# The last stage of a float32 decoder trunk: where h is turned token-major

## The chip, the cores and the metric

The kernel runs on one core of a Trainium2 chip. The metric is the device time of one execution in microseconds (us). Three runs of the kernel before took 1103.12 to 1103.98, median 1103.35.

## The reference, cut to what matters

Two layers over 512 tokens of 1024 features, in float32: differential attention or multi-scale pooling, a gated MLP with a short convolution, and a gated per-layer embedding. The change is in the last of these, together with the final norm:

```
for i in range(DEPTH):
    ...
    h = h + conv_glu_ffn(rmsnorm(h, ffn_norm_g[i]), w_up[i], conv_w[i], conv_b[i], w_down[i])
    gate = jax.nn.sigmoid(rmsnorm(h, ple_norm_g[i]) @ w_ple_gate[i])
    h = h + gate * (p[i] @ w_ple_proj[i])
return rmsnorm(h, final_norm_g)
```

## The kernel before, in words

The order of each engine's instructions is written by hand; semaphores join the engines. Through most of the kernel h is feature-major: `h[:, k, :]` holds 128 features (partitions) of tile k for all 512 tokens. Every product is made of three TensorE instructions (lines 1257 to 1259): the high parts, and each low part with the other's high part. Weights come in units of 128x1024 float32 into four slots (`w_raw`, loaded from SyncE, line 340); ScalarE makes the high part (`split_hi`, line 392), VectorE the low part (`split_lo`, line 821).

The last down phase of the MLP (`residual_phase("down12", ...)`) adds eight tiles to h. For each tile VectorE makes the low part of a coming weight unit (line 821), adds the result to h (line 1038), makes the low part of the normed input of the tile before (`x_low`, line 829) and adds its squares up (`sum_squares`, line 856). ScalarE makes the input's high part and the squares between them.

The last stage is different: its output is token-major. The gate product has 128 tokens as rows and 512 of the 1024 output features as columns, and it runs in two halves of the features. In the first half k, the tile of input features, is the outer loop, and the four token tiles t share the banks 0 to 3: 8 steps of 4 x 3 = 12 matmuls. After k = 1 stand the token sums of the norm (`norm_sums`, line 1277). In the second half t is the outer loop; the last t is cut into two pieces of 256 columns. The stage's weights are 8 units, TAIL to TAIL+7. To add h, it must be token-major as well: `h_tok`, eight pieces of 128 tokens by 512 features. `token_transposes` (line 1628) makes each with four TensorE transposes of 128x128 into a bank, ScalarE copies it to SBUF (line 683).

Behind the products ScalarE makes the sigmoid (`gate`, line 704), VectorE multiplies it with the embedding (`gated`, line 1207) and adds `h_tok` (line 1209), ScalarE sums the squares (lines 711, 718), GpSimd makes the inverse root (lines 806 to 810), and VectorE scales and multiplies with the gain (`final`, line 1220), from where SyncE stores. For the last token tile the gain is multiplied in early (line 1230), and ScalarE scales (line 752). GpSimd has done nothing else since the pooling masks at 244 us. It has issued transfers only in the attention (lines 779 and 783).

`h_tok` lies over the buffers `g_hi` and `g_lo`, which the down phase reads.

Of the kernel before, what the change touches and what calls it, by code (L numbers as in the profile page):

```python
# [8 lines left out]
F32 = mybir.dt.float32  # L9
# [24 lines left out]
PLE_KT = PLE_DIM // P  # L34
POOL_KT = D_MODEL // len(POOL_WINDOWS) // P
GROUP = SEQ // P
N_GROUPS = N_HEADS // GROUP
ROW_HEADS = N_HEADS - 2
FFN_PARTS = (8, 8, 6)
# [57 lines left out]
def hybrid_trunk(nc, gain_and_x0, xT, pT, weights, final_gain, columns, out, o_rows):  # L97
    with ExitStack() as ctx:
        def sem(name):
            return ctx.enter_context(nc.semaphore(name))  # L100

        def sb(name, shape, dt, scope=ctx):
            return scope.enter_context(nc.sbuf_tensor(name, shape, dt))
# [19 lines left out]
        p_raw = sb("p_raw", [P, DEPTH * PLE_KT, SEQ], F32, product)  # L123
        product.close()
        product = ExitStack()
        h_tok = sb("h_tok", [P, 2 * TT, SEQ], F32, product)
        product.close()
        g_hi = sb("g_hi", [P, KT, SEQ], F32R)
        g_lo = sb("g_lo", [P, KT, SEQ], F32R)
# [44 lines left out]

        gain_b = sb("gain_b", [P, D_MODEL], F32, ffn)
        G = len(POOL_WINDOWS)
        band32 = sb("band32", [P, G, BAND], F32, ffn)
        edge32 = sb("edge32", [P, G, EDGE], F32, ffn)
        band = sb("band", [P, G, BAND], F32R, ffn)
        first_band = sb("first_band", [P, G, BAND], F32R, ffn)  # L180
        edge_lo = sb("edge_lo", [P, G, EDGE], F32R, ffn)
        mlp = ExitStack()
        u32 = sb("u32", [P, 2, PAD + SEQ], F32, mlp)
        c32 = sb("c32", [P, 2, SEQ], F32, mlp)
# [48 lines left out]
            sem("band_one"), sem("band_below"), sem("band_set"), sem("band_diff"), sem("band_done"), sem("edge_done"))  # L233
        z_mm, zhi_done, zlo_done, pool_mm = sem("z_mm"), sem("zhi_done"), sem("zlo_done"), sem("pool_mm")

        h_T, h_copied, gate_mm, gate_done, gated_done, h_added = (
            sem("h_T"), sem("h_copied"), sem("gate_mm"), sem("gate_done"), sem("gated_done"), sem("h_added"))
        first_sq, second_sq, last_sq, token_total, token_var, frms_done, finv_done, gain_in, gained_done = (
            sem("first_sq"), sem("second_sq"), sem("last_sq"), sem("token_total"), sem("token_var"), sem("frms_done"),
            sem("finv_done"), sem("gain_in"), sem("gained_done"))  # L240
# [83 lines left out]
        def z_bank(i):  # L324

            return bank[4 + (i + 1) % 3]

        WO_BANKS = (1, 0, 7, 3)
        WT_BANKS = [(0, 512), (512, 384), (896, 384)]
# [53 lines left out]
        def _(act):  # L383
# [294 lines left out]
                add_pool_bias(KT - 1)  # L678


            def tokens_copy(m):
                act.wait_ge(h_T, m + 1)
                act.activation(h_tok[:, m, :], bank[4 + m % 3][:, :], ACT.Copy).then_inc(h_copied, 1)

            gates = [g32, s32]

            tables = iter(range(104, 116))
# [18 lines left out]
            def first_square(t):  # L706

                act.wait_ge(h_added, t + 1)
                if t:
                    act.wait_ge(first_sq, t)  # L710
                act.activation(u32[:, 0, 0:SEQ], h_tok[:, t, :], ACT.Square, accum_out=first_sum[:, t:t + 1]).then_inc(first_sq, 1)

            def second_square(t):

                act.wait_ge(h_added, TT + t + 1)
                if t:
                    act.wait_ge(second_sq, t)
                act.activation(u32[:, 1, 0:SEQ], h_tok[:, TT + t, :], ACT.Square,
                               accum_out=second_sum[:, t:t + 1]).then_inc(second_sq, 1)

            split_hi(TAIL + 2)
            split_hi(TAIL + 3)
            rms_of(NORM_PLE1)
            split_hi(TAIL + 4)
            for m in range(4):
                tokens_copy(m)
            split_hi(TAIL + 5)
            for m in range(4, 8):
                tokens_copy(m)
            split_hi(TAIL + 6)  # L730
            table(ACT.Sigmoid)
            act.wait_ge(icol_done, NORM_PLE1 + 1)
# [25 lines left out]
        def _(pool):  # L758
# [38 lines left out]
            for mat, width in ((band32, BAND), (edge32, EDGE)):  # L797

                for g, win in enumerate(POOL_WINDOWS):
                    pool.affine_select(out=mat[:, g, :], in_=mat[:, g, :], compare_op=ALU.is_ge, fill=0.0, base=win - 1,  # L800
                                       pattern=[[-1, width]], channel_multiplier=1).then_inc(band_set, 1)

            for t in range(TT - 1):
                pool.wait_ge(first_sq, t + 1)
# [9 lines left out]
        def _(dve):  # L814
            def split_lo(n, a=0):

                if n >= N_UNITS:
                    return
                s, w = slot_of(n), blocks_of(n) * P
                dve.wait_ge(hi_done, SLOTS * a + n + 1)  # L820
                dve.tensor_tensor(w_lo[s][:, 0:w], w_raw[s][:, 0:w], w_hi[s][:, 0:w].bitcast(F32),  # L821
                                  ALU.subtract).then_inc(lo_done, 1)
# [28 lines left out]
            def sum_squares(norm, m):  # L851
                n_sq = KT * norm + m
                dve.wait_ge(sq_done, n_sq + 1)
                if m:
                    dve.wait_ge(acc_done, n_sq)
                    dve.tensor_tensor(acc[:, :], acc[:, :], sq[:, n_sq % 2, :], ALU.add).then_inc(acc_done, 1)
                else:
                    dve.tensor_copy(acc[:, :], sq[:, n_sq % 2, :]).then_inc(acc_done, 1)
# [178 lines left out]
            def residual_add(m, src):  # L1037
                dve.tensor_tensor(h[:, m, :], src, h[:, m, :], ALU.add).then_inc(evac_done, 1)  # L1038

            def residual_phase(name, norm, layer, which, look=LOOK):  # L1040
                for m in range(KT):
                    n = PHASES[name][0] + m
                    if m + look < KT + LOOK:
                        split_lo(n + look)
                    dve.wait_ge(unit_done, n + 1)
                    residual_add(m, bank[WO_BANKS[m % SLOTS] if name == "wo" else m % SLOTS][:, :])
                    if norm is not None and m > 0:
                        x_low(norm, m - 1, gain(layer, which, m - 1))
                        sum_squares(norm, m - 1)
                if norm is not None:  # L1050
                    x_low(norm, KT - 1, gain(layer, which, KT - 1))
                    sum_squares(norm, KT - 1)
# [142 lines left out]

            split_lo(TAIL + 2)
            split_lo(TAIL + 3)
            inverse(NORM_PLE1)
            for n in range(4, 8):
                split_lo(TAIL + n)  # L1200
# [2 lines left out]
            def gated(i):  # L1203

                m, cols = PIECES[i]
                dve.wait_ge(gate_done, i + 1)
                dve.tensor_tensor(c32[:, i % 2, cols], emb[:, m, cols], gates[i % 2][:, cols], ALU.mult).then_inc(gated_done, 1)  # L1207
                dve.wait_ge(gated_done, i + 1)
                dve.tensor_tensor(h_tok[:, m, cols], c32[:, i % 2, cols], h_tok[:, m, cols], ALU.add).then_inc(h_added, 1)  # L1209

            def last_square(i, before, into):

                m, cols = PIECES[i]
                dve.wait_ge(h_added, i + 1)
                dve.tensor_tensor_reduce(c32[:, i % 2, cols], h_tok[:, m, cols], h_tok[:, m, cols], 1.0, before,
                                         ALU.mult, ALU.add, into).then_inc(last_sq, 1)

            def final(m, cols=slice(0, SEQ)):
                half, t = divmod(m, TT)
                dve.scalar_tensor_tensor(out=emb[:, m, cols], in0=h_tok[:, m, cols], scalar=final_inv[:, t:t + 1],  # L1220
                                         in1=gain_b[:, half * SEQ + cols.start:half * SEQ + cols.stop],
                                         op0=ALU.mult, op1=ALU.mult).then_inc(y_dve, 1)

            dve.wait_ge(h_copied, 2 * TT)
            dve.wait_ge(emb_done, DEPTH * KT)
            for t in range(TT):
                gated(t)
            dve.wait_ge(gain_in, 16)
            dve.wait_ge(h_added, TT)
            dve.tensor_tensor(emb[:, TT - 1, :], h_tok[:, TT - 1, :], gain_b[:, 0:SEQ], ALU.mult).then_inc(gained_done, 1)  # L1230
            for t in range(TT - 1):
                gated(TT + t)
                if t == TT - 2:
# [17 lines left out]
        def _(pe):  # L1251
# [365 lines left out]
                return exact(dst, [((x_hi[:, k, TOK[t]], x_lo[:, k, TOK[t]]), (w_hi[s][:, w], w_lo[s][:, w]), no_wait)],  # L1617
                             start=k == 0, stop=k == KT - 1)

            def token_transposes(m):  # L1620

                half, t = divmod(m, TT)
                if m >= 3:
                    pe.wait_ge(h_copied, m - 2)
                else:
                    pe.wait_ge(emb_done, DEPTH * KT)
                for j in range(TT):
                    last = pe.transpose(bank[4 + m % 3][:, j * P:(j + 1) * P], h[:, half * TT + j, TOK[t]], ident[:, :])
                last.then_inc(h_T, 1)

            for k in range(KT):
                pe.wait_ge(lo_done, TAIL + k // 2 + 1)
                pe.wait_ge(x_ready, KT * NORM_PLE1 + k + 1)
                for t in range(TT):
                    if k == 0:
                        pe.wait_ge(evac_done, result_of("down12", TT + t))
                    done = gate_product(bank[t][:, :], 0, k, t)
                    if k % 2 and t == TT - 1:
                        done.then_inc(unit_done, 1)
                    elif k == KT - 1:  # L1640
                        done.then_inc(gate_mm, 1)
                if k == 1:
                    norm_sums(NORM_PLE1)
                if 2 <= k < 6:
                    token_transposes(2 * k - 4)
                    token_transposes(2 * k - 3)

            pe.wait_ge(h_copied, 2 * TT)
            pe.wait_ge(rms_done, NORM_PLE1 + 1)
            for t in range(TT - 1):  # L1650
                for k in range(KT):
# [93 lines left out]
```

## Time and profile before

| | us |
|---|---|
| median of three runs | 1103.35 |
| profiled execution | 1103.46 |
| its span, first to last instruction | 1101.7 |
| TensorE busy in the span | 1089.8 (99%) |
| VectorE busy | 719.2 (65%) |
| ScalarE busy | 515.0 (47%) |
| GpSimd busy | 25.2 (2%) |

Busy time is no time on the path. What sets the end is read from the chain that ended last, and what an engine waits for from the idle time ahead of an instruction. Matmuls overlap in the pipeline, so their durations add up to more than the time between their starts. The granted clock of TensorE was 0.998 of full speed.

### The profile page before, as it was taken

The page shows a single profiled execution, that of the slowest core. Times are in us where ns is not written, and L with a number is a line of the kernel's source. Part 1 is how long each engine was busy: PE and PEld are TensorE (multiplying, and loading weights), DVE is VectorE, ACT ScalarE, POOL GpSimd, SP SyncE. Part 2 cuts the span into 40 slices and gives each one's busy share as a digit, 9 for nine tenths or more (in the row PEclk, how much of TensorE's full clock was granted, in tenths as well). Part 3 has the DMA queues.
Part 4 walks back from the last instruction along what each step waited for, and adds up shares of the span by engine and source line. Part 5 has one row for each costly group of instructions (what it writes and reads, how often), then busy time and mean ns, then how long its engine had stood idle before and what let it go on. Part 6 is the DMA issues. An engine that isn't in the chain of part 4 may idle for free.

```text
span 1101.7 us, 14447 instructions
## 1 busy us (share of the span) xinstructions
PE 1089.8 (99%) x5152; PEld 908.5 (82%) x5152; DVE 719.2 (65%) x1107; ACT 515.0 (47%) x775; POOL 25.2 (2%) x82
## 2 busy tenths in 40 slices
PE   9999999999999999999999999999999999999997
PEld 8878888888888888888888888888888888888886
DVE  7567878575775377743776778777437773477636
ACT  6456667364643144421445677444314442244554
POOL 0001110020000000000000000000000000000001
PEclk9999999999999999999999999999999999999999
DMA  8213243233233233232233222233322233233411
GB/s 330 62 58 83 62 96 79 65 109 103 92 99 115 77 95 95 96 115 79 95 103 127 95 94 77 77 95 99 114 78 101 95 106 115 77 95 95 134 58 76
DMA packets 31295, 107.88 MB, mean 98 GB/s; under 512 B 3600, under 2 KB 3600, under 8 KB 31248
## 3 DMA queue, kind: packets, MB, share of 16 engines
q1 hardware_dynamic: 30288, 105.13, 30.8%
q0 software_dynamic: 672, 1.59, 0.6%
q8 instruction: 30, 0.49, 0.2%
q10 hardware_dynamic: 288, 0.53, 0.2%
q14 instruction: 17, 0.14, 0.0%
HBM read 105.12 MB, written 2.11 MB: 97 GB/s over the span
## 4 chain that ended last, share of the span: by engine, by line
PE 93%; DVE 4%; ACT 2%; issue 1%; POOL 0%; DVEq 0%; ACTq 0%; POOLq 0%
PE bank L1257 29%; PE bank L1259 29%; PE bank L1258 29%; PE bank L1351 1%; PE bank L1277 1%; DVE w_lo L821 1%; PE bank L1364 1%; DVE probs L943 1%; DVE h_tok L1209 1%; DVE c L1207 0%; ACT probs L494 0%; DVE emb L1220 0%; PE bank L1318 0%; ACT w_hi L392 0%; PE bank L1544 0%
## 5 line engine op out<-in xcount | busy, mean ns | idle before, releaser
L1257 PE MATMUL bank<-x_hi,w_hi 128*128 128x512 f32 x896 | 350.2, 391 | 0.0
L1259 PE MATMUL bank<-x_hi,w_lo 128*128 128x512 f32 x896 | 348.8, 389 | 0.0
L1258 PE MATMUL bank<-x_lo,w_hi 128*128 128x512 f32 x896 | 348.7, 389 | 0.0
L821 DVE TENSOR_TENSOR w_lo<-w_raw,w_hi 128x1024 fp32r<-128x1024 f32 (+1 forms) x189 | 226.0, 1197 | 52.6 <-ACT w_hi L392 52.5
L392 ACT ACTIVATE w_hi<-w_raw 128x1024 fp32r<-128x1024 f32 (+1 forms) x189 | 193.8, 1031 | 109.4 <-PE bank L1259 109.4
L1259 PEld LDWEIGHTS bank<-x_hi,w_lo 128*128 128x128 f32 x896 | 168.2, 188 | 35.0
L1257 PEld LDWEIGHTS bank<-x_hi,w_hi 128*128 128x128 f32 x896 | 168.2, 188 | 34.8 <-issue 0.4
L1258 PEld LDWEIGHTS bank<-x_lo,w_hi 128*128 128x128 f32 x896 | 168.3, 188 | 34.5
L1257 PE MATMUL bank<-g_hi,w_hi 128*128 128x512 f32 x352 | 136.9, 389 | 0.0
L1258 PE MATMUL bank<-g_lo,w_hi 128*128 128x512 f32 x352 | 136.9, 389 | 0.0
L1259 PE MATMUL bank<-g_hi,w_lo 128*128 128x512 f32 x352 | 136.9, 389 | 0.0
L637 ACT ACTIVATE c<-u,params 128x512 f32<-128x512 f32 x88 | 71.8, 816 | 106.7 <-DVE u L1132 106.7
L1132 DVE TENSOR_TENSOR u<-bank,inv 128x512 f32<-128x512 f32 x88 | 60.7, 689 | 92.2 <-PE bank L1259 92.1
L1038 DVE TENSOR_TENSOR gain_and_h<-bank,gain_and_h 128x512 f32<-128x512 f32 x56 | 38.5, 688 | 97.9 <-PE bank L1259 97.9
L644 ACT ACTIVATE g_hi<-g 128x512 f32 (+1 forms) x44 | 27.8, 632 | 118.8 <-DVE g L1148 118.8
L1257 PEld LDWEIGHTS bank<-g_hi,w_hi 128*128 128x128 f32 x352 | 66.1, 188 | 13.8
L1258 PEld LDWEIGHTS bank<-g_lo,w_hi 128*128 128x128 f32 x352 | 66.1, 188 | 13.7
L1259 PEld LDWEIGHTS bank<-g_hi,w_lo 128*128 128x128 f32 x352 | 66.1, 188 | 13.6
L1142 DVE SCALAR_TENSOR_TENSOR c<-u,params,c 128x512 f32<-128x512 f32 x88 | 66.2, 752 | 10.3 <-DVE c L1137 2.1
L1137 DVE SCALAR_TENSOR_TENSOR c<-u,params,c 128x512 f32<-128x512 f32 x88 | 66.0, 750 | 2.3 <-ACT c L637 0.9
L642 ACT ACTIVATE s<-c 128x512 f32<-128x512 f32 x44 | 27.8, 632 | 75.2 <-DVE c L1142 75.2
L1150 DVE TENSOR_TENSOR g_lo<-g,g_hi 128x512 f32 (+1 forms) x44 | 30.5, 693 | 38.1 <-ACT g_hi L644 38.1
(218 smaller groups left out, 1172.7 us busy)
## 6 DMA issues: line engine op xcount, KB each, us to landing
w_raw<-in_weights SPq DMA_DIRECT2D x189, 512.0 KB, 3.5
gain_and_h<-in_xT SPq DMA_DIRECT2D x7, 256.0 KB, 5.6
o_inv<-o_rows POOLq DMA_DIRECT2D x6, 256.0 KB, 4.8
out<-emb SPq DMA_DIRECT2D x3, 512.0 KB, 3.0
p_raw<-in_pT SPq DMA_DIRECT2D x1, 1024.0 KB, 10.0
w_raw<-in_weights SPq DMA_DIRECT2D x2, 256.0 KB, 3.7
gain_b<-in_final_gain SPq DMA_DIRECT2D x1, 512.0 KB, 4.0
gain_and_h<-in_gain_and_x ACTq DMA_DIRECT2D x1, 260.0 KB, 3.6
```

The costliest lines, as they stand in the source:

```text
L392: act.activation(w_hi[s][:, 0:w], w_raw[s][:, 0:w], ACT.Copy).then_inc(hi_done, 1)
L637: act.activation(c32[:, c, :], u32[:, c, PAD:PAD + SEQ], ACT.Identity, scale=tap(layer, 2, j + c * FT), bias=conv_bias(layer, j + c * FT)) ...
L642: act.activation(s32[:, :], c32[:, 0, :], ACT.Silu).then_inc(silu_done, 1)
L821: dve.tensor_tensor(w_lo[s][:, 0:w], w_raw[s][:, 0:w], w_hi[s][:, 0:w].bitcast(F32), ALU.subtract).then_inc(lo_done, 1)
L1038: dve.tensor_tensor(h[:, m, :], src, h[:, m, :], ALU.add).then_inc(evac_done, 1)
L1132: dve.tensor_tensor(u32[:, c, PAD:], bank[2 * v + c][:, :], inv[:, :], ALU.mult).then_inc(evac_done, 1)
L1137: dve.scalar_tensor_tensor(out=c32[:, c, :], in0=u32[:, c, PAD - 1:PAD - 1 + SEQ], scalar=tap(layer, 1, j + c * FT), in1=c32[:, c, :], op0 ...
L1142: dve.scalar_tensor_tensor(out=c32[:, c, :], in0=u32[:, c, PAD - 2:PAD - 2 + SEQ], scalar=tap(layer, 0, j + c * FT), in1=c32[:, c, :], op0 ...
L1150: dve.tensor_tensor(g_lo[:, 2 * a + v, :], g32[:, :], g_hi[:, 2 * a + v, :].bitcast(F32), ALU.subtract).then_inc(glo_done, 1)
L1257: pe.matmul(dst, w1, m1, start=start and i == 0, stop=False)
L1258: pe.matmul(dst, w1, m0, start=False, stop=False)
L1259: last = pe.matmul(dst, w0, m1, start=False, stop=stop and i == len(parts) - 1)
```

## The change

The TensorE transposes and ScalarE's copies are taken out. VectorE transposes each tile of h in 32x32 blocks into a new buffer, `turned`, once it is done; a block lands on the 32 partitions from which it came. GpSimd then issues 16 transfers within SBUF, each of which carries the blocks of one quarter of the partitions (a) that belong to one quarter of the tokens (c) to their partitions. A run is 4 x 32 elements (512 bytes) on the reading side; a transfer has 32 partitions of 8 runs. `h_tok` has another order within a partition, so the sum reads it in runs of 32 elements; it is written to `emb`, which all that follows reads. `turned` takes the place of the pooling masks.

```
+        turned = sb("turned", [P, KT, P // SQUARE, TT, SQUARE], F32, ffn)
...
+        def h_token_major(m, cols):
+            half, t = divmod(m, TT)
+            tiles = slice(half * TT + cols.start // P, half * TT + cols.stop // P)
+            return h_tok[:, :, tiles, t, :].rearrange("p a j x -> p j a x")
...
-            for m in range(4):
-                tokens_copy(m)
             split_hi(TAIL + 5)
-            for m in range(4, 8):
-                tokens_copy(m)
...
+            pool.wait_ge(unit_done, TAIL)
+            pool.wait_ge(h_turned, KT)
+            for c in range(P // SQUARE):
+                for a in range(P // SQUARE):
+                    pool.dma_start(h_tok[c * SQUARE:(c + 1) * SQUARE, a, :, :, :],
+                                   turned[a * SQUARE:(a + 1) * SQUARE, :, c, :, :]).then_inc(h_moved, 16)
...
+            def turn(m):
+                dve.wait_ge(evac_done, result_of("down12", m))
+                dve.transpose(turned[:, m, :, :, :].rearrange("p c t x -> p t c x"), h[:, m, :].rearrange("p (t c x) -> p t c x", t=TT, x=SQUARE)).then_inc(h_turned, 1)
...
                         sum_squares(norm, m - 1)
+                        if norm == NORM_PLE1:
+                            turn(m - 1)
...
             split_lo(TAIL + 3)
+            turn(KT - 1)
             inverse(NORM_PLE1)
...
-                dve.tensor_tensor(h_tok[:, m, cols], c32[:, i % 2, cols], h_tok[:, m, cols], ALU.add).then_inc(h_added, 1)
+                by_tile = "p (j a x) -> p j a x"
+                dve.tensor_tensor(emb[:, m, cols].rearrange(by_tile, a=P // SQUARE, x=SQUARE),
+                                  c32[:, i % 2, cols].rearrange(by_tile, a=P // SQUARE, x=SQUARE),
+                                  h_token_major(m, cols), ALU.add).then_inc(h_added, 1)
...
-            dve.wait_ge(h_copied, 2 * TT)
+            dve.wait_ge(h_moved, 16 * (P // SQUARE) ** 2)
...
-            dve.wait_ge(h_added, TT)
-            dve.tensor_tensor(emb[:, TT - 1, :], h_tok[:, TT - 1, :], gain_b[:, 0:SEQ], ALU.mult).then_inc(gained_done, 1)
+            dve.wait_ge(first_sq, TT)
+            dve.tensor_tensor(emb[:, TT - 1, :], emb[:, TT - 1, :], gain_b[:, 0:SEQ], ALU.mult).then_inc(gained_done, 1)
...
-                if 2 <= k < 6:
-                    token_transposes(2 * k - 4)
-                    token_transposes(2 * k - 3)
-
-            pe.wait_ge(h_copied, 2 * TT)
+            pe.wait_ge(emb_done, DEPTH * KT)
```

VectorE before, from the low part and the residual sum of the last tile to the low parts of the gate's units:

```order
L821 TENSOR_TENSOR w_lo<-w_raw,w_hi 128x1024 [waits hi_done]
L1038 TENSOR_TENSOR gain_and_h<-bank,gain_and_h 128x512 [waits unit_done]
L829 SCALAR_TENSOR_TENSOR x_lo<-gain_and_h,params,x_hi 128x512 [waits xhi_done]
L856 TENSOR_TENSOR acc<-acc,sq 128x512 [waits acc_done,sq_done]
L829 SCALAR_TENSOR_TENSOR x_lo<-gain_and_h,params,x_hi 128x512 [waits xhi_done]
L856 TENSOR_TENSOR acc<-acc,sq 128x512 [waits acc_done,sq_done]
L821 TENSOR_TENSOR w_lo<-w_raw,w_hi 128x1024 [waits hi_done] x2
L846 RECIPROCAL small<-small 128x4 [waits rms_done]
```

And the same place now (lines are some ten further down):

```order
L830 TENSOR_TENSOR w_lo<-w_raw,w_hi 128x1024 [waits hi_done]
L1047 TENSOR_TENSOR gain_and_h<-bank,gain_and_h 128x512 [waits unit_done]
L838 SCALAR_TENSOR_TENSOR x_lo<-gain_and_h,params,x_hi 128x512 [waits xhi_done]
L865 TENSOR_TENSOR acc<-acc,sq 128x512 [waits acc_done,sq_done]
L1052 STREAM_TRANSPOSE turned<-gain_and_h 128x4x4x32 [waits evac_done]
L838 SCALAR_TENSOR_TENSOR x_lo<-gain_and_h,params,x_hi 128x512 [waits xhi_done]
L865 TENSOR_TENSOR acc<-acc,sq 128x512 [waits acc_done,sq_done]
L830 TENSOR_TENSOR w_lo<-w_raw,w_hi 128x1024 [waits hi_done] x2
L1052 STREAM_TRANSPOSE turned<-gain_and_h 128x4x4x32 [waits evac_done]
L855 RECIPROCAL small<-small 128x4 [waits rms_done]
```

Turn 6 stands ahead of the last tile's low part and sum of squares, turn 7 behind the low parts of two weight units; turns 0 to 5 stand one in each tile before.

ScalarE before, from the high part of unit TAIL+4 to the first two sigmoids:

```order
L392 ACTIVATE w_hi<-w_raw 128x1024 [waits unit_done,raw_in2]
L683 ACTIVATE h_tok<-bank 128x512 [waits h_T] x4
L392 ACTIVATE w_hi<-w_raw 128x1024 [waits unit_done,raw_in3]
L683 ACTIVATE h_tok<-bank 128x512 [waits h_T] x4
L392 ACTIVATE w_hi<-w_raw 128x1024 [waits unit_done,raw_in0]
L691 ACT_TABLE_LOAD
L691 ACTIVATE small<-eps 128x1
L392 ACTIVATE w_hi<-w_raw 128x1024 [waits unit_done,raw_in1,icol_done]
L704 ACTIVATE g<-bank,small 128x512 [waits gate_mm]
L704 ACTIVATE s<-bank,small 128x512 [waits gate_mm]
```

Now the eight copies are gone; the order of the rest is kept. On GpSimd the transfers stand behind the masks and ahead of the inverse roots:

```order
L802 AFFINE_SELECT band<-band 128x144 x3
L802 AFFINE_SELECT edge<-edge 128x16 x4
L809 DMA h_tok<-turned 32x8x128 [waits h_turned,unit_done]
L809 DMA h_tok<-turned 32x8x128 x15
L815 TENSOR_TENSOR small<-small 128x1 [waits second_sq,first_sq]
L817 TENSOR_SCALAR small<-small 128x1 [waits token_total]
L819 TENSOR_TENSOR small<-small 128x1 [waits token_var]
```

Nothing of the kernel's own is queued behind them on GpSimd until the first inverse root.

## Rows read from the trace of the kernel before

**Rows 1.** The page's chain that ended last, by engine:

```profile
PE 93%; DVE 4%; ACT 2%; issue 1%; POOL 0%; DVEq 0%; ACTq 0%; POOLq 0%
```

**Rows 2.** The chain in order of time, last stage: start, us, what:

```profile
1054.52 0.87 PE bank L1628 x8
...
1071.86 1.06 ACT w_hi L392
...
1074.09 0.70 DVE c L1207
...
1083.74 0.58 POOL small L810
...
1084.35 1.42 DVE emb L1220 x2
```

**Rows 3.** The line of the transposes: duration ns min/median/max, starts:

```profile
L1628 PE MATMUL bank<-ident,gain_and_h x32: 270/272/273, 1054.4 to 1066.0; 128*128 128x128 f32 x32
```

**Rows 4.** Timeline of TensorE: start, us, engine line op, count, idle before:

```profile
1050.73 0.95 PE L1277 MATMUL bank<-ones,acc 128*128 128x1 f32 x8
...
1051.54 0.48 PE L1257 MATMUL bank<-w_hi,x_hi 128*128 128x512 f32 x1
...
1054.36 1.03 PE L1628 MATMUL bank<-ident,gain_and_h 128*128 128x128 f32 x8
...
1071.58 0.39 PE L1257 MATMUL bank<-w_hi,x_hi 128*128 128x512 f32 x1
...
1074.30 0.39 PE L1257 MATMUL bank<-w_hi,x_hi 128*128 128x512 f32 x1
```

**Rows 5.** VectorE's groups by shape: busy us, mean ns, idle before:

```profile
L821 DVE TENSOR_TENSOR w_lo<-w_raw,w_hi 128x1024 fp32r<-128x1024 f32 x173 | 210.7, 1219 | 41.6 <-ACT w_hi L392 41.6
...
L858 DVE COPY acc<-sq 128x512 f32<-128x512 f32 x6 | 2.5, 420 | 0.0
```

**Rows 6.** Timeline of VectorE, end of the down phase:

```profile
1037.40 0.96 DVE L821 TENSOR_TENSOR w_lo<-w_raw,w_hi 128x768 fp32r<-128x768 f32 x1 [0.79 <-ACT w_hi L392]
...
1046.46 0.68 DVE L1038 TENSOR_TENSOR gain_and_h<-bank,gain_and_h 128x512 f32<-128x512 f32 x1
...
1048.32 0.74 DVE L829 SCALAR_TENSOR_TENSOR x_lo<-gain_and_h,params,x_hi 128x512 fp32r<-128x512 f32 x1
1048.98 0.68 DVE L856 TENSOR_TENSOR acc<-acc,sq 128x512 f32<-128x512 f32 x1
1049.59 2.35 DVE L821 TENSOR_TENSOR w_lo<-w_raw,w_hi 128x1024 fp32r<-128x1024 f32 x2
```

**Rows 7.** Waits of TensorE's loads, 1045 to 1095 us: total, times, longest:

```profile
PEld bank L1257 <- DVE gain_and_h L1038: 0.2, 1, 0.2
```

**Rows 8.** GpSimd's transfers in the attention, by line: issue in ns, landing in us:

```profile
L779 POOL DMA_DIRECT2D o_rows<-small x6: 595/600/752, 85.3 to 171.5; - x6
...
DMA to landing us min/median/max: 1.7/1.7/1.9
...
L783 POOL DMA_DIRECT2D o_inv<-o_rows x6: 536/542/557, 87.5 to 173.5; - x6
...
DMA to landing us min/median/max: 4.4/4.8/5.4
```

**Rows 9.** Busy time by stretch, last three: granted clock, DMA share, GB/s:

```profile
1054.00:1058.00 4.00, 4.00 (x24) 3.33 (x23) 0.26 (x1) 1.09 (x2) 0.00 (x0) 1.00 0.31 119
1058.00:1071.50 13.50, 13.50 (x73) 11.49 (x72) 2.45 (x2) 6.64 (x10) 0.00 (x0) 1.00 0.00 1
```

**Rows 10.** Timelines of VectorE and ScalarE around the early gain:

```profile
1079.60 0.69 DVE L1230 TENSOR_TENSOR emb<-h_tok,gain_b 128x512 f32<-128x512 f32 x1
1080.06 0.19 ACT L711 ACTIVATION_READ_ACCUMULATOR u<-h_tok 128x1 f32 x1
1080.86 0.69 DVE L1207 TENSOR_TENSOR c<-emb,g 128x512 f32<-128x512 f32 x1 [0.57 <-ACT g L704]
```

**Rows 11.** The page's DMA issues: KB each, us to landing:

```profile
w_raw<-in_weights SPq DMA_DIRECT2D x189, 512.0 KB, 3.5
```

More of the change, by code:

```diff
@@ L36 @@
 GROUP = SEQ // P
+SQUARE = 32
 N_GROUPS = N_HEADS // GROUP
@@ L125, in hybrid_trunk @@
         product = ExitStack()
-        h_tok = sb("h_tok", [P, 2 * TT, SEQ], F32, product)
+        h_tok = sb("h_tok", [P, P // SQUARE, KT, TT, SQUARE], F32, product)
         product.close()
@@ L176, in hybrid_trunk @@
         G = len(POOL_WINDOWS)
[L177 to L181, printed above, removed]
+        pooling = ExitStack()
+        band32 = sb("band32", [P, G, BAND], F32, pooling)
+        edge32 = sb("edge32", [P, G, EDGE], F32, pooling)
+        band = sb("band", [P, G, BAND], F32R, pooling)
+        first_band = sb("first_band", [P, G, BAND], F32R, pooling)
+        edge_lo = sb("edge_lo", [P, G, EDGE], F32R, pooling)
+        pooling.close()
+        turned = sb("turned", [P, KT, P // SQUARE, TT, SQUARE], F32, ffn)
         mlp = ExitStack()
@@ L234, in hybrid_trunk @@
         z_mm, zhi_done, zlo_done, pool_mm = sem("z_mm"), sem("zhi_done"), sem("zlo_done"), sem("pool_mm")
-        h_T, h_copied, gate_mm, gate_done, gated_done, h_added = (
-            sem("h_T"), sem("h_copied"), sem("gate_mm"), sem("gate_done"), sem("gated_done"), sem("h_added"))
+        h_turned, h_moved, gate_mm, gate_done, gated_done, h_added = (
+            sem("h_turned"), sem("h_moved"), sem("gate_mm"), sem("gate_done"), sem("gated_done"), sem("h_added"))
         first_sq, second_sq, last_sq, token_total, token_var, frms_done, finv_done, gain_in, gained_done = (
@@ L678, in _ @@
                 add_pool_bias(KT - 1)
-            def tokens_copy(m):
-                act.wait_ge(h_T, m + 1)
-                act.activation(h_tok[:, m, :], bank[4 + m % 3][:, :], ACT.Copy).then_inc(h_copied, 1)
             gates = [g32, s32]
@@ L710, in first_square @@
                     act.wait_ge(first_sq, t)
-                act.activation(u32[:, 0, 0:SEQ], h_tok[:, t, :], ACT.Square, accum_out=first_sum[:, t:t + 1]).then_inc(first_sq, 1)
+                act.activation(u32[:, 0, 0:SEQ], emb[:, t, :], ACT.Square, accum_out=first_sum[:, t:t + 1]).then_inc(first_sq, 1)
             def second_square(t):
@@ L717, in second_square @@
                     act.wait_ge(second_sq, t)
-                act.activation(u32[:, 1, 0:SEQ], h_tok[:, TT + t, :], ACT.Square,
+                act.activation(u32[:, 1, 0:SEQ], emb[:, TT + t, :], ACT.Square,
                                accum_out=second_sum[:, t:t + 1]).then_inc(second_sq, 1)
@@ L1214, in last_square @@
                 dve.wait_ge(h_added, i + 1)
-                dve.tensor_tensor_reduce(c32[:, i % 2, cols], h_tok[:, m, cols], h_tok[:, m, cols], 1.0, before,
+                dve.tensor_tensor_reduce(c32[:, i % 2, cols], emb[:, m, cols], emb[:, m, cols], 1.0, before,
                                          ALU.mult, ALU.add, into).then_inc(last_sq, 1)
@@ L1219, in final @@
                 half, t = divmod(m, TT)
-                dve.scalar_tensor_tensor(out=emb[:, m, cols], in0=h_tok[:, m, cols], scalar=final_inv[:, t:t + 1],
+                dve.scalar_tensor_tensor(out=emb[:, m, cols], in0=emb[:, m, cols], scalar=final_inv[:, t:t + 1],
                                          in1=gain_b[:, half * SEQ + cols.start:half * SEQ + cols.stop],
                                          op0=ALU.mult, op1=ALU.mult).then_inc(y_dve, 1)
-            dve.wait_ge(h_copied, 2 * TT)
+            dve.wait_ge(h_moved, 16 * (P // SQUARE) ** 2)
             dve.wait_ge(emb_done, DEPTH * KT)
@@ L1618, in gate_product @@
                              start=k == 0, stop=k == KT - 1)
[L1620 to L1629, printed above, removed]
             for k in range(KT):
```

## The prediction

> **What bounds the kernel now.** I read the chain that ended last first: 93% of the span is TensorE, so an instruction taken out of TensorE's row is worth its full length, unless something else becomes late [rows 1]. Then the chain inside the last stage. Up to 1071.8 us it runs through TensorE, and a group of eight transposes (0.87 us) is a link of it; at 1071.86 it passes to ScalarE's copy of the last weight unit and from there, at 1074.09, to VectorE, where it stays with short steps on ScalarE and GpSimd [rows 2]. The reader is to see that the tail after 1074 does not wait for TensorE's second half: it is one chain that starts where the first half of the gate product ends. Whatever moves that point moves the end by as much, if the token-major h is there when VectorE asks for it.
>
> **What the change takes from TensorE.** 32 transposes stand in four groups of eight [rows 3]. The duration of one (272 ns) is pipelined and does not add up, so I take starts. From the first matmul of k = 2 (1051.54) to the first of the second half (1071.58) are 20.04 us [rows 4]. They hold six steps of 12 matmuls; undisturbed, 12 take 1074.30 - 1071.58 = 2.72 us, six take 16.32. The rest, 3.72, is the four groups and the slower start after each pause. A slower start of 0.1 us follows the token sums too, and stays (k = 2 takes 2.82 from 1051.54 to 1054.36, where nothing but the sums stands ahead). So 3.6 us go. TensorE waits for no copy inside this stretch, and the eight ScalarE copies that go were off the chain.
>
> **What it adds on VectorE.** Eight 32x32 transposes of 128x512. The trace has no such instruction. Near rows of 128x512 take 0.42 us (copy, [rows 5]) and 0.68 (sum, [rows 6]); the far end is 1.22 for 1024 columns [rows 5]. I take 0.69, in a full queue some 0.6, as the sum's successor starts 0.6 after it. Seven are put behind the sum of squares of their tile in the last down phase, where VectorE is idle 0.79 us before the next low part, which waits for ScalarE [rows 6] (so three times; 1.0 us before the other low parts). At 0.6 they fit and move nothing. At 1.22, in a full queue 1.15, three turns would be 0.36 too long and three 0.1 to 0.15, and this would reach TensorE, for its k = 0 step already waited 0.2 us for the last residual sum [rows 7]: 1.5 us back. Below nothing it can't be: nothing goes from VectorE here. Queued behind turn 6 are the last low part and sum of squares. The sum of squares, ended at about 1049.6, now ends at about 1050.2, and TensorE takes it at 1050.73, after k = 1; the low part is used by k = 7, some 15 us later. Turn 7 stands behind two low parts of weights: 1049.59 + 2.3 + 0.6 is 1052.5, and it ends at about 1053.2. The reciprocal and the low part behind it come up to 1.2 us later; the sigmoids that use the first start near 1069, and the unit of the second is used from 1068 on.
>
> **The transfers.** GpSimd waits for turn 7, then issues 16 transfers of 32 partitions, 128 KB each, in runs of 512 bytes, 256 of them in each. VectorE's first token-major sum now waits for all 16. It would ask 1074.09 - 3.6 = 1070.5. With c the time from one transfer to the next and L the landing of the last, they are there at 1053.3 + 15c + L, so the room is 15c + L = 17.2 us. What stands behind this wait is the whole tail, so any excess counts fully.
> The nearest rows are GpSimd's own transfers in the attention [rows 8]: the issue took 0.54 to 0.75 us for 128 partitions of one run, the landing 1.7 us for 2 KB and 4.8 for 256 KB from HBM. Lower end: c = 0.54, L = 1.7: 9.8 us. If the issue grows with the runs, c is twice 0.6 = 1.2. Upper ends: if they land one after another, c = 1.7, and by the far row c = 4.8 (77 us). For c I take the middle between an issue that does not grow and one that doubles, 0.9; for L 2.2, the 1.7 and 0.5 for 128 KB. Sum: 1053.3 + 13.5 + 2.2 = 1069.0. That is 1.5 us early, and the transfers cost nothing. Their cover is TensorE's steps k = 2 to 7; the DMA engines are empty then (1 GB/s from 1058 to 1071.5, [rows 9]), so only the last weight units, on their way until 1058, share them.
> [...]
>
> **The tail.** The token-major sum writes emb and reads h_tok in runs of 32 elements, the rest reads emb. Number and length of the instructions stay (0.69 us); a strided read may add up to 0.05 each on six of the chain, which no row of before shows; I take nothing. One wait is new: the multiplication by the gain (L1230) is in place and must follow ScalarE's fourth square. It started at 1079.60; that square is read out at 1080.25 [rows 10]. So it runs from 1080.28 to 1080.9, and the next gated product, which started at 1080.86, waits for it: 0.05 to 0.1 us. I take 0.1.
>
> **Sum.** -3.6 + 0.1 = -3.5 us, on the profiled execution's 1103.46 (span 1101.7 and 1.8 around it): 1100.0. The median shown is 0.1 below that execution, so 1099.9; with something for the strided reads I say 1100.0.
>
> **Rivals.**
> A wait for the transfers that eats the gain. If the issue goes with the number of runs, c = 1.2: 1053.3 + 18 + 2.2 = 1073.5, 3.0 late, net -0.5: 1102.9. [...] Against: 2 KB and 256 KB were issued in the same 0.6 us, so part of it is fixed. This case is c from 1.07 to 1.4, 1100.5 to 1105.5.
> Slower: the transfers take turns. From c = 1.4 on (3.5 us of gain and 2.2 more) the end is worse than before. With the landing of 1.7 us as the pace they are there at 1053.3 + 25.5 + 2.2 = 1081.0, 10.5 late, net +7: 1110.4. [...] Against: a weight load moves 512 KB in 3.5 us from issue to landing [rows 11], so 2 MB of bytes alone are no 25 us.
> VectorE's transpose is slow. At 1.22 us it gives 1.5 back: 1101.5. Against: both near rows are below 0.7.
> The transposes were hidden anyway: 1103.4. The chain names them, so I give it little.
>
> **Chances.** Forecast 0.49 (1099.3 to 1100.5), issue-bound 0.20, taking turns 0.23, slow transpose 0.05, no effect 0.03. What this measurement can tell from no change is about 0.2%, 2.2 us: faster is below 1101.1, slower above 1105.6. Faster: 0.49, 0.04 of the second, 0.02 of the fourth: 0.55. Slower 0.23; the rest, 0.22, same. The range goes from 1099.2 to 1110.5: it leaves out the half of the third case above its middle, and the likeliest case's own range is 1099.3 to 1100.5.
>
> **What the profile after would show.** TensorE: second half starts at 1068.0 instead of 1071.6, no pause between k = 2 and 7. VectorE: eight transposes of 0.6 to 0.75 us, the idle time before the low parts shrunk from 0.8 to 0.1 or 0.2, the last residual sum still at 1046.5. GpSimd: 16 issues from 1053.3, the last one before 1068; their spacing is c. VectorE's first gated product at 1070.5, released by ScalarE. If it is released by a DMA, the forecast is wrong by exactly that wait; if the spacing exceeds 1.1 us, the first or second rival holds.

## The result and the profile after

The changed kernel takes 1109.22 us (median of six, 1108.29 to 1109.85) against 1103.38 before: ratio 1.0051, interval 1.004 to 1.0062. It is slower by 5.8 us, where 3.4 less were forecast. The forecast was wrong in sign; its second rival, the transfers that take turns, had 1110.4.

| | after | change |
|---|---|---|
| span of the profiled execution, us | 1107.7 | +6.0 |
| TensorE busy | 1086.3 | -3.5 |
| VectorE busy | 723.8 | +4.6 |
| GpSimd busy | 34.6 | +9.4 |

The waits of the last stage come first (engine, line, waited for whom, total, times, longest):

```profile
POOL h_tok L809 <- issue: 14.7, 5, 4.6
...
DVE c L1224 <- DMA h_tok<-turned: 9.3, 1, 9.3
...
PEld bank L1277 <- DVE gain_and_h L1047: 0.2, 1, 0.2
```

The middle one is the result: VectorE stands still for 9.3 us until the transfers are there. The last is the same 0.2 as before [rows 7]: the transposes on VectorE did not reach TensorE. The first shows where the time went, but not why: GpSimd stopped five times between its transfers, and no semaphore of the kernel released it. Its timeline (start, us, line, count, idle time before):

```profile
1054.17 1.80 POOL L809 DMA_DIRECT2D h_tok<-turned  x3 [809.69 <-DVE turned L1052]
1060.61 1.75 POOL L809 DMA_DIRECT2D h_tok<-turned  x3 [4.63 <-issue]
1064.66 1.74 POOL L809 DMA_DIRECT2D h_tok<-turned  x3 [2.31 <-issue]
1068.43 1.73 POOL L809 DMA_DIRECT2D h_tok<-turned  x3 [2.03 <-issue]
1072.53 1.74 POOL L809 DMA_DIRECT2D h_tok<-turned  x3 [2.37 <-issue]
1077.65 0.58 POOL L809 DMA_DIRECT2D h_tok<-turned  x1 [3.38 <-issue]
```

Three at a time, then a gap. The issues take 8.8 us up to the last one, the gaps 14.7, the last landing 2.3: 25.8 us. With the 0.9 us that pass between the end of turn 7 (1053.3) and the first issue it is 26.7, where there was room for 17.2. The line of the transfers, by source, gives issue and landing, as [rows 8] did for those of the attention:

```profile
L809 POOL DMA_DIRECT2D h_tok<-turned x16: 582/583/632, 1054.2 to 1077.7; - x16
...
DMA to landing us min/median/max: 2.2/2.6/4.8
```

VectorE, the same places as [rows 6], [rows 2] and [rows 10]:

```profile
1037.52 0.96 DVE L830 TENSOR_TENSOR w_lo<-w_raw,w_hi 128x768 fp32r<-128x768 f32 x1 [0.17 <-ACT w_hi L402]
...
1046.57 0.68 DVE L1047 TENSOR_TENSOR gain_and_h<-bank,gain_and_h 128x512 f32<-128x512 f32 x1
...
1052.57 0.70 DVE L1052 STREAM_TRANSPOSE turned<-gain_and_h 128x512 f32<-128x512 f32 x1
...
1079.95 0.69 DVE L1224 TENSOR_TENSOR c<-emb,g 128x512 f32<-128x512 f32 x1 [9.30 <-DMA h_tok<-turned]
1080.67 0.69 DVE L1227 TENSOR_TENSOR emb<-c,h_tok 128x512 f32<-128x512 f32 x1
...
1086.21 0.69 DVE L1250 TENSOR_TENSOR emb<-emb,gain_b 128x512 f32<-128x512 f32 x1 [0.86 <-ACT u L717]
1086.82 0.69 DVE L1224 TENSOR_TENSOR c<-emb,g 128x512 f32<-128x512 f32 x1
```

The idle time ahead of the low part shrank from 0.79 to 0.17, the last residual sum moved by 0.1, the transpose takes 0.70. The sum that reads `h_tok` in runs of 32 elements (L1227) takes 0.69, as its predecessor did without the strides. And TensorE, as [rows 4], from k = 2 to the second half:

```profile
1051.63 0.48 PE L1277 MATMUL bank<-w_hi,x_hi 128*128 128x512 f32 x1
...
1068.05 0.39 PE L1277 MATMUL bank<-w_hi,x_hi 128*128 128x512 f32 x1
```

16.42 us instead of 20.04: the 3.6 us are gone as worked out. The balance: -3.6, +0.1 for the early gain, and 9.4 for the wait make +5.9; the spans differ by 6.0. (Without the wait the first product would have started at 1070.6, 3.5 us before its old 1074.09, since the second half starts 3.5 earlier.)

The wait stands ahead of the first product (L1224), which reads no `h_tok`; only the sum behind it does. Placed ahead of the sum it would have cost some 0.7 us less, an estimate from the starts 1079.95 and 1080.67. That was not tried.

### The profile page after: what moved, and what is told of

Read it like the earlier page. It is cut to its first block, busy times and chain, and to the rows that moved or that the text cites. A ratio compares the mean times of both kernels' runs of the same rounds, so it can differ in the third digit from the quotient of the medians.

```text
span 1107.7 us, 14400 instructions
## 1 busy us (share of the span) xinstructions
PE 1086.3 (98%) x5120; PEld 905.4 (82%) x5120; DVE 723.8 (65%) x1115; ACT 510.8 (46%) x767; POOL 34.6 (3%) x98
## 2 busy tenths in 40 slices
DMA packets 32063, 109.98 MB, mean 99 GB/s; under 512 B 3856, under 2 KB 3856, under 8 KB 32016
## 4 chain that ended last, share of the span: by engine, by line
PE 87%; DVE 5%; issue 3%; ACT 3%; POOL 1%; DMA 0%; DVEq 0%; POOLq 0%; ACTq 0%
PE bank L1277 28%; PE bank L1278 28%; PE bank L1279 28%; PE bank L1371 1%; DVE w_lo L830 1%; PE bank L1297 1%; POOL h_tok L809 1%; ACT w_hi L402 1%; PE bank L1384 1%; DVE probs L952 1%; DVE gain_and_h L1047 1%; DVE emb L1227 1%; DVE c L1224 0%; ACT probs L504 0%; ACT sq L563 0%
```

## The experiments

The kernel is built with a reserve of 1024 bytes, the line `dynamic_dma_scratch_size=1024`. Three theories for the gaps stood against each other. R: GpSimd's transfers take room in this reserve, more of it with more runs, and three of 256 runs fill it (an expectation below calls it the ring). P: the bytes, 32 partitions at a time, bind. T: GpSimd keeps three transfers in flight, whatever their size.

The changed kernel's own trace already speaks against P. This is the DMA engines' busy share from 1060 to 1064 us and from 1064 to 1068, in slices of 0.1 us:

```profile
DMA  0000000000000000079939539949800149966600
```

```profile
DMA  0000000000000000009959424997964939700000
```

The engines stand empty from 1063.8 to 1065.8, ahead of and behind the start of the next group at 1064.66: GpSimd did not wait for room on them.

**Without the transfers.** VectorE's sum reads the blocks that VectorE wrote.

```
-            return h_tok[:, :, tiles, t, :].rearrange("p a j x -> p j a x")
+            return turned[:, tiles, :, t, :]
...
-            pool.wait_ge(unit_done, TAIL)
-            pool.wait_ge(h_turned, KT)
-            for c in range(P // SQUARE):
-                for a in range(P // SQUARE):
-                    pool.dma_start(h_tok[c * SQUARE:(c + 1) * SQUARE, a, :, :, :],
-                                   turned[a * SQUARE:(a + 1) * SQUARE, :, c, :, :]).then_inc(h_moved, 16)
...
-            dve.wait_ge(h_moved, 16 * (P // SQUARE) ** 2)
+            dve.wait_ge(h_turned, KT)
```

> The 16 GpSimd transfers are left out and VectorE's sum reads the transposed blocks from where its own transposes wrote them (the same strides' kind, runs of 32), so its numbers are another function's. All else is the changed kernel. This is the sum of the prediction without the transfers: -3.6 us of TensorE, +0.1 for the wait ahead of the early gain. Theory A (all of the loss is the wait for the transfers): 1099.8 to 1100.3 us, the first gated product at 1070.4 to 1070.6. Rival B (part of the loss is elsewhere, in strided reads or in VectorE's transposes): above 1101.

Measured: 1099.91 us (1099.6 to 1100.58), ratio 0.9967, 0.9955 to 0.9979; the first gated product starts at 1070.31. What the forecast said of the rest of the kernel holds: the whole loss is the wait for the transfers, and strided reads cost nothing that shows (the sum takes 0.69 us here too).

**Runs of 4096 bytes.**

```
-        turned = sb("turned", [P, KT, P // SQUARE, TT, SQUARE], F32, ffn)
+        turned = sb("turned", [P, P // SQUARE, KT, TT, SQUARE], F32, ffn)
...
-                dve.transpose(turned[:, m, :, :, :].rearrange("p c t x -> p t c x"), ...
+                dve.transpose(turned[:, :, m, :, :].rearrange("p c t x -> p t c x"), ...
...
-                                   turned[a * SQUARE:(a + 1) * SQUARE, :, c, :, :]).then_inc(h_moved, 16)
+                                   turned[a * SQUARE:(a + 1) * SQUARE, c, :, :, :]).then_inc(h_moved, 16)
```

> The buffer of the transposed blocks is laid out with the token quarter outermost, so each of the 16 transfers reads one run of 4096 bytes a partition instead of eight of 512. Same bytes, same partitions, same count, same issuing engine. [...] Rival P (the bytes of 32 partitions at a time bind the DMA engines or SBUF's ports): no change, 1109. Rival T (GpSimd keeps three transfers in flight whatever their size): groups of three stay, 1108 to 1109.

Measured: 1099.89 us (1099.53 to 1100.54), ratio 0.9966, 0.9952 to 0.9979. Theory R's forecast was no gap between the issues, all landed before 1068, 1099.8 to 1100.5 us. GpSimd's timeline, VectorE's and the line of the transfers:

```profile
1053.78 7.81 POOL L809 DMA_DIRECT2D h_tok<-turned  x16 [809.42 <-DVE turned L1052]
...
1069.37 1.23 DVE L830 TENSOR_TENSOR w_lo<-w_raw,w_hi 128x1024 fp32r<-128x1024 f32 x1 [4.24 <-ACT w_hi L402]
1070.51 0.68 DVE L1224 TENSOR_TENSOR c<-emb,g 128x512 f32<-128x512 f32 x1
...
L809 POOL DMA_DIRECT2D h_tok<-turned x16: 489/492/533, 1053.8 to 1061.1; - x16
...
DMA to landing us min/median/max: 4.8/6.7/8.3
```

All 16 are issued in 7.8 us without a gap, and VectorE goes on at 1070.51 without a wait. The bytes, the partitions, the count and the issuing engine are unchanged, and so is what VectorE does beside them, so P and T fall: under T three would be in flight, here ten had been issued when the first landed (1053.78 + 4.8). Under R, ten on their way in 1024 bytes mean at most 102 bytes for one transfer of 32 runs, an estimate. This version beats both kernels, by 3.8 us against the one before measured beside it (1103.72). The landing of one grows to 6.7 us, and by the last issue and the longest landing all is there at 1069.4: hidden, but later than theory R's 1068, and with 1.1 us to spare.

**Same number of runs, a quarter of the bytes.** VectorE's sum reads its own blocks as in the first experiment, but still waits for all 16 transfers. In these:

```
-                    pool.dma_start(h_tok[c * SQUARE:(c + 1) * SQUARE, a, :, :, :],
-                                   turned[a * SQUARE:(a + 1) * SQUARE, :, c, :, :]).then_inc(h_moved, 16)
+                    pool.dma_start(h_tok[c * SQUARE:(c + 1) * SQUARE, a, :, 0:1, :],
+                                   turned[a * SQUARE:(a + 1) * SQUARE, :, c, 0:1, :]).then_inc(h_moved, 16)
...
             dve.wait_ge(h_moved, 16 * (P // SQUARE) ** 2)
+            dve.wait_ge(h_turned, KT)
```

> Each run carries 128 bytes instead of 512 (a quarter of h is moved, the rest left out, and VectorE's sum reads VectorE's own blocks as in e1, so the numbers are another function's; it still waits for all 16). [...] Theory R: groups of three stay and the gaps shrink only by what the bytes take, under 1 us each: 1104 to 1109. Rival P: the transfers are four times as quick, no gap: 1100. Rival T: as R.

Measured: 1102.93 us (1102.28 to 1106.06), ratio 0.9998, 0.9989 to 1.0008. Two of its ten runs took 1106.1, the other eight at most 1103.6.

```profile
1054.65 1.81 POOL L809 DMA_DIRECT2D h_tok<-turned  x3 [809.72 <-DVE turned L1052]
1058.99 1.75 POOL L809 DMA_DIRECT2D h_tok<-turned  x3 [2.53 <-issue]
1062.36 1.75 POOL L809 DMA_DIRECT2D h_tok<-turned  x3 [1.62 <-issue]
```

The groups of three stay with a quarter of the bytes, as R says and P does not. But the time is 1.1 us below the range given for R: the five gaps are 8.8 us in all instead of 14.7, and the first and the last shrank by 2.1 and 1.8, where less than 1 each was expected. So of the changed kernel's gaps some 6 us go with the bytes, which lengthen the landings (median 1.8 us here, 2.6 there), and 9 stay with a quarter of them.

**The size of the reserve.** One line, `dynamic_dma_scratch_size=1024`, with 512, 1536 and 1152.

> [...] Theory R: issues stand alone, one each 2.4 to 3 us, the last landed after some 43 us instead of 26: about 1126. Rivals P and T: 1109.

Measured with 512 bytes: 1125.69 us, one run.

> [...] Theory R: issues in groups of five, five, five and one; three gaps instead of five, each of 2 to 3 us (the first longer), so the last lands some 4 to 5 us earlier than in the changed kernel: 1104 to 1105.5. Rival T (three in flight whatever the reserve): no change, 1108.5 to 1109.5.

Measured with 1536 bytes: 1105.62 us (1105.27 to 1106.16), ratio 1.0018, 1.0008 to 1.0027.

> [...] Theory R: four groups of four, three gaps: last issue at 1069 to 1072 instead of 1077.7, time 1104 to 1107.

Measured with 1152 bytes: 1106.29 us, one run. Two rows of GpSimd with 512 bytes, then with 1536:

```profile
1060.53 0.58 POOL L809 DMA_DIRECT2D h_tok<-turned  x1 [1.94 <-issue]
1063.09 0.59 POOL L809 DMA_DIRECT2D h_tok<-turned  x1 [1.97 <-issue]
```

```profile
1053.93 2.97 POOL L809 DMA_DIRECT2D h_tok<-turned  x5 [809.51 <-DVE turned L1052]
1062.65 2.89 POOL L809 DMA_DIRECT2D h_tok<-turned  x5 [5.75 <-issue]
1068.06 2.89 POOL L809 DMA_DIRECT2D h_tok<-turned  x5 [2.52 <-issue]
1073.55 0.58 POOL L809 DMA_DIRECT2D h_tok<-turned  x1 [2.60 <-issue]
```

| reserve, bytes | groups seen | room of one transfer, bytes | us |
|---|---|---|---|
| 512 | 16 of 1 | over 256, up to 512 | 1125.7 |
| 1024 | 5 of 3, 1 | over 256, up to 341 | 1109.2 |
| 1152 | 4 of 4 | over 230, up to 288 | 1106.3 |
| 1536 | 3 of 5, 1 | over 256, up to 307 | 1105.6 |

The third column is an estimate from the first two: if a group is as many transfers as the reserve holds, one takes at most the reserve over their number, and more than the reserve over one more. All four rows agree on more than 256 and up to 288 bytes for a transfer of 256 runs. The groups came as expected, but the room from which I foretold five and four had been shown by no run; the three in 1024 bytes alone leave it between 256 and 341. The packets do not show it either: 3856 are under 512 bytes where there were 3600, 16 more for each of the 16 transfers, but it is 3856 with the runs of 4096 bytes too. That the edit touches nothing but the reserve shows that its size sets the groups, and T falls a second time. The last issue with 1152 came at 1072.3, a little later than the 1069 to 1072 expected. With 1536 the time is 0.1 us above the range: fewer gaps, but the first is longer (5.75); five transfers are then on their way beside the last weight loads, which is the likely reason. A reserve that holds all 16 (16 x 288 = 4608 bytes at most, by the same estimate) was not tried.

**Issued from SyncE.** Both waits and the 16 transfers, unchanged, stand on SyncE behind the last weight load.

> The 16 transfers with runs of 512 bytes are issued from SyncE's queue, behind its last weight load, instead of GpSimd's. Nothing else changes. Theory R (the ring is GpSimd's own): no groups, one issue each 0.33 to 0.6 us, all landed before 1068: 1099.8 to 1100.5. Rival (runs of 512 bytes are slow in themselves, whoever issues them): the last lands later than 1072 and the time is above 1101.5.

Measured: 1100.32 us (1100.05 to 1101.1), ratio 0.9969, 0.9957 to 0.998. SyncE's timeline and the line of the transfers:

```profile
1053.24 11.06 SPq L381 DMA_DIRECT2D h_tok<-turned  x16
...
L381 SPq DMA_DIRECT2D h_tok<-turned x16: 611/622/887, 1053.2 to 1063.7; - x16
...
DMA to landing us min/median/max: 5.9/6.0/6.6
```

No groups, one issue each 0.69 us on average, a little above what was expected, and VectorE's first product at 1070.33, as without the transfers (1070.31). So nine or so are in flight at a time with the same runs of 512 bytes, and the groups belong to GpSimd's way of issuing. But it is close: the last transfer landed at 1063.7 + 6.6 = 1070.3, not before 1068 as expected, just when VectorE asked.

**Another order of the transfers**, on top of the long runs:

```
-            for c in range(P // SQUARE):
-                for a in range(P // SQUARE):
+            for turn_by in range(P // SQUARE):
+                for c in range(P // SQUARE):
+                    a = (c + turn_by) % (P // SQUARE)
```

> The kernel with runs of 4096 bytes (e2), its 16 transfers in another order: neighbours in the queue differ in both the partitions they read and those they write, where before four in a row wrote the same 32. In e2 the transfers moved about 200 GB/s. Theory S (the same 32 partitions bound that pace): above 300 GB/s and all landed 4 us or more earlier than in e2 (some 1065 instead of 1069). Rival (the pace is that of the transfers' own work): as e2. Both: time as e2, 1099.8 to 1100.2, since they land before VectorE asks.

Measured: 1100.34 us (1099.83 to 1100.74), ratio 0.9967, 0.9955 to 0.998: as the long runs. What the DMA engines moved from 1060 to 1072, in 40 slices (busy tenths, GB/s), without and with the new order:

```profile
DMA  9999999999998999998997676461000000000000
GB/s 205 219 219 219 205 219 219 219 219 219 219 205 178 273 219 219 205 219 178 205 191 150 150 164 137 96 137 27 0 0 0 0 0 0 0 0 0 0 0 0
```

```profile
DMA  9999999999999999997576430000000000000000
GB/s 219 232 246 219 219 219 232 219 301 260 232 232 246 219 246 219 219 219 164 137 178 164 109 82 14 0 0 0 0 0 0 0 0 0 0 0 0 0 0 0
```

Theory S (that writes to the same 32 partitions bound the pace) fails: the pace rises from about 215 to about 230, not above 300, with all engines busy in both. It ends 0.9 us earlier though it began 0.8 later (issues from 1054.6 instead of 1053.8). That neighbours write the same 32 partitions seems to cost a little, by one profiled execution of each; what holds the pace near 220 GB/s stays open. That one transfer reaches 32 partitions only is a candidate which no run here varied.

## Why the prediction was wrong

- *TensorE, -3.6 us*: right. 20.04 became 16.42, and the kernel without the transfers ran at 1099.91 where 1100.0 was the sum. The strided reads, for which 0.05 each was named on no row and nothing taken, cost nothing (0.69 before and after).
- *VectorE's transposes fit into the idle time*: right, 0.70 us each; idle 0.79 became 0.17, and TensorE's wait for the last residual sum stayed at 0.2. The rival of a slow transpose is out.
- *The early gain, +0.1*: right. The product behind it started at 1086.82, 0.61 after the gain, while its sigmoid had ended at 1086.68.
- *The tail is one chain that follows its first product*: right. 9.4 us of wait minus 3.5 are 5.9, and that is the loss.
- *The transfers, 1053.3 + 15c + L with c = 0.9*: this is the step that failed. Here c was to be "the middle between an issue that does not grow and one that doubles". The issue did not grow (0.58 for 256 runs, 0.49 for 32), so the first rival's mechanism is out too. But c is not the issue: measured, c is (1077.65 - 1054.17) / 15 = 1.57, of which 0.58 is issue and 0.98 are the gaps. I asked only what one transfer costs GpSimd, and not how many can be on their way and what happens when no more can.
- *L = 2.2 and a start at 1053.3*: the 0.5 for 128 KB in L stood on no row; transfers of 32 KB landed in 1.8 us (the run with a quarter of the bytes), of 128 KB in 2.3 (that with 512 bytes of reserve; medians). L fits the last transfer (2.3), but the first group took 4.6 to 4.8 us to land. Until 1058 the last weight units were on their way, which the forecast named and priced at nothing. The start was 0.9 later than said: turn 7 ended at 1053.27 and is what the trace names as releaser, but the first issue came at 1054.17; in the other runs that issued from GpSimd the same step took 0.6 to 0.9 us, from SyncE 0.2. What GpSimd does in it is open.
- *The taking of turns*, with 0.23: right in its place and in the point from which it decides (c = 1.4), but by another count. Three go together and then nothing for 2 to 4.6 us, where I had each wait 1.7 for the one before. That its price came near (+7 for +5.8) is luck: its 15 x 1.7 = 25.5 stands against 23.5, and these are 8.8 of issues and 14.7 of gaps.
- *How many can be on their way.* The sum has no term for it, and no row of before shows it; the groups of three do. Yet by itself a limit of three gives no loss. If a landed transfer made room for the next, three in flight with a landing of 2.2 us are one each 0.73, and all is there in time. If a group must land whole, it is 5 x (1.2 + 2.2) + 2.2 = 19.2 us, 2.0 late: 1101.9, still faster than before. The measured 26.7 needed the rest: 0.9 for the late start, 0.35 from each landing to the next issue (1.8), the first group's landing (2.6), and the later landings, of up to 3.6 where 2.2 was taken (2.3 in all). The 3.6 stands beside a load of 16 KB of instructions at 1073.8; that it is the reason was not tested.
- *The signs that were named* read true: the spacing is above 1.1, the first product is released by a DMA, and its wait of 9.3 is the distance between 1100.0 and 1109.2 within 0.1. A bound was slightly off: by the sum's own terms c = 1.07 gives 1101.0, and the 1100.5 stated for it belongs to 1.03. Nothing hangs on it.

## What to carry to other kernels

Many transfers of many runs on GpSimd's queue have two prices: the issue (0.58 us each here), and the room that they take in the reserve. Here one of 256 runs took more than 256 and up to 288 bytes, the estimate from the four reserves, and one of 32 runs at most 102; other numbers of runs were not measured. Divide the reserve by the room of one, and set a whole landing and 0.35 us between the groups; only what fits goes back to back. Take the landing from a row with as much traffic beside it. Make the runs longer before anything else, since that cost one swapped dimension here and turned a loss of 5.8 us into a gain of 3.8; or issue from SyncE, where no such groups showed, but where the last landing came just in time.

## What the runs showed of the hardware

- A group was not followed by single transfers, one for each landing. GpSimd went on only when the whole group had landed: in the second group the first transfer, issued at 1060.61, landed 2.3 us later at 1062.9, and nothing was issued on it; the third issue is at 1061.77, it landed 2.55 later at 1064.32, and the next group starts at 1064.66. So it was in all 31 gaps of the five runs with groups of one, three, four or five: the next issue came 0.30 to 0.39 us after the last landing. Why is open.
- The profile shows this wait as "issue", without a releaser (14.7 us, 5 times, with 1024 bytes). Rows of GpSimd's transfers in equal groups with such gaps were the sign here.
- 256 runs of 512 bytes were issued in 0.58 us and 32 runs of 4096 in 0.49: what a run adds to GpSimd's issue is below a nanosecond.
- Copies within SBUF ran at some 215 GB/s with all 16 DMA engines busy, each of 32 partitions, while weight loads of the kernel before, of 128 partitions, reach 426 in a slice of 0.75 us (down phase). Hidden here, it would be the next bound: 2 MB are some 10 us, an estimate from the 215.
